# Query pieces of a weight-streaming kernel: one 512-column product and one 256-column product in place of three of 256 columns

## What is computed

```python
def peer(h, w_query, sub_keys, u_experts, v_experts):
    tokens = h.reshape(B * S // PEER_CHUNK, PEER_CHUNK, D)
    def chunk(xc):
        qh = (xc @ w_query).reshape(PEER_CHUNK, PEER_HEADS, PEER_QDIM)
        s1 = jnp.einsum('thd,hnd->thn', qh[..., :PEER_HALF], sub_keys[:, 0])
        s2 = jnp.einsum('thd,hnd->thn', qh[..., PEER_HALF:], sub_keys[:, 1])
        v1, i1 = lax.top_k(s1, PEER_TOPK)
        v2, i2 = lax.top_k(s2, PEER_TOPK)
        ...
        z = jnp.einsum('td,thkd->thk', xc, u_experts[idx])
        ...
```

## Time and profile before

| what | value |
|---|---|
| timed runs, median (lowest, highest) | 1732.64 us (1731.53, 1732.9) |
| profiled execution, span | 1732.8 us |
| TensorE matmul busy | 1711.1 us, 99% |
| weight loads busy | 1580.1 us, 91% |
| VectorE busy | 1328.8 us, 77% |
| ScalarE busy | 925.9 us, 53% |
| mean granted TensorE clock | 0.996 |

### The profile page before, as it was taken

How to read it: one execution, slowest core, us unless ns; L and a number is a source line. 1 busy time by engine, 2 the same in 40 slices (tenths; PEclk the granted TensorE clock), 3 DMA queues, 4 the chain that set the end, 5 groups by cost and what they waited for, 6 DMA issues and landing times.

```text
span 1732.8 us, 33390 instructions
## 1 busy us (share of the span) xinstructions
PE 1711.1 (99%) x11670; PEld 1580.1 (91%) x11670; DVE 1328.8 (77%) x2382; ACT 925.9 (53%) x1647; POOL 63.5 (4%) x112
## 2 busy tenths in 40 slices
PE   9999999999999999999999999999999999999997
PEld 8899899989999898999889999999999988888886
DVE  6986778778976787877775999987888766666666
ACT  5444544445454544455554555577777655555553
POOL 0000001000000122100000000000000000000000
PEclk9999999999999999999999999999999999999999
DMA  6556687755445699744344555554444455555554
GB/s 232 170 179 199 217 291 274 244 181 167 162 159 161 226 328 308 253 148 145 122 158 158 166 175 182 182 171 136 145 135 137 144 194 194 193 192 192 191 192 153
DMA packets 90123, 327.30 MB, mean 189 GB/s; under 512 B 11001, under 2 KB 11177, under 8 KB 89585
## 3 DMA queue, kind: packets, MB, share of 16 engines
q1 hardware_dynamic: 79056, 286.45, 49.3%
q0 software_dynamic: 9712, 34.36, 6.2%
q10 hardware_dynamic: 1264, 5.24, 0.8%
HBM read 323.88 MB, written 6.09 MB: 190 GB/s over the span
## 4 chain that ended last, share of the span: by engine, by line
PE 76%; DVE 18%; DMA 2%; issue 2%; ACT 2%; DVEq 0%; ACTq 0%; SPq 0%
PE bank L210 23%; PE bank L211 22%; PE bank L212 22%; DVE Z L87 6%; DVE w_lo L187 6%; PE bank L1769 3%; DMA raw<-stream 1%; DVE yc L87 1%; PE bank L281 1%; PE bank L1310 1%; ACT w_hi L182 1%; PE bank L481 1%; DVE work L87 1%; DVE rot L87 1%; DVE top L87 1%
## 5 line engine op out<-in xcount | busy, mean ns | idle before, releaser
L187 DVE TENSOR_TENSOR w_lo<-raw,w_hi 128x1024 fp32r<-128x1024 f32 x544 | 658.2, 1220 | 162.1 <-ACT w_hi L182 161.2
L182 ACT ACTIVATE w_hi<-raw 128x1024 fp32r<-128x1024 f32 x544 | 572.4, 1054 | 245.5 <-PE bank L212 163.2
L210 PE MATMUL bank<-u_hi,w_hi 128*128 128x256 f32 x2400 | 691.2, 288 | 1.7 <-DVE w_lo L187 0.8
L211 PE MATMUL bank<-u_lo,w_hi 128*128 128x256 f32 x2400 | 679.8, 283 | 0.0
L212 PE MATMUL bank<-u_hi,w_lo 128*128 128x256 f32 x2400 | 679.7, 283 | 0.0
L210 PEld LDWEIGHTS bank<-u_hi,w_hi 128*128 128x128 f32 x2400 | 460.9, 192 | 11.6 <-DVE w_lo L187 3.8
L211 PEld LDWEIGHTS bank<-u_lo,w_hi 128*128 128x128 f32 x2400 | 461.2, 192 | 2.2
L212 PEld LDWEIGHTS bank<-u_hi,w_lo 128*128 128x128 f32 x2400 | 460.7, 192 | 0.0
L210 PE MATMUL bank<-w_hi,a_hi 128*128 128x512 f32 x744 | 290.4, 390 | 0.0
L211 PE MATMUL bank<-w_lo,a_hi 128*128 128x512 f32 x744 | 290.1, 390 | 0.0
L212 PE MATMUL bank<-w_hi,a_lo 128*128 128x512 f32 x744 | 289.5, 389 | 0.0
(11 more groups left out here) (286 smaller groups left out, 1713.1 us busy)
## 6 DMA issues: line engine op xcount, KB each, us to landing
raw<-stream SPq DMA_DIRECT2D x544, 512.0 KB, 3.3
gate<-w_ada POOLq DMA_DIRECT2D x48, 512.0 KB, 6.4
t_rows<-t_by_distance POOLq DMA_DIRECT2D x8, 256.0 KB, 3.4
rpb_rows<-rpb_pad POOLq DMA_DIRECT2D x8, 224.0 KB, 3.9
bias_b<-rpb_rows POOLq DMA_DIRECT2D x16, 96.0 KB, 7.7
bias_a<-t_rows POOLq DMA_DIRECT2D x1, 1536.0 KB, 14.9
x<-x_in ACTq DMA_DIRECT2D x2, 512.0 KB, 5.8
gains_b<-gains POOLq DMA_DIRECT2D x1, 1024.0 KB, 9.0
```

The lines of the kernel that those rows point to most:

```text
L182: nc.scalar.activation(w_hi[:, s, :], raw[:, s, :], ACT.Copy).then_inc(s_hi, 1)
L187: nc.vector.tensor_tensor(w_lo[:, s, :], raw[:, s, :], w_hi[:, s, :].bitcast(F32), ALU.subtract).then_inc(s_split, 1)
L210: M.matmul(o, lh, rh, start=start, stop=False, skip_group_check=True)
L211: M.matmul(o, lh, rl, start=False, stop=False, skip_group_check=True)
```

## The change

`u_hi` and `u_lo` become the two halves of one tile, `u_hl`, so that for each k-step the high and the low part stand side by side as 512 columns. For the query pieces alone, three matmuls a k-step become two: `w_hi` times both parts in one matmul of 512 columns, which fills a whole bank, and `w_lo` times the high part, 256 columns, added to the bank's upper half. The result is the sum of the bank's halves: ScalarE copies the lower half out and VectorE adds the upper one to it. Each query piece has a bank of its own: q0 and q1 banks 4 and 5 as before, then bank `4 + (f + e - 1) % 4` for piece f + e, which is 5, 6, 7, 4, 5, 6, 7, 4 and so on for q2, q3, ... . All other products read `u_hi` and `u_lo` as views of the new tile.

```diff
-        u_hi = sb(ctx, "u_hi", [P, KD, T], F32R)
-        u_lo = sb(ctx, "u_lo", [P, KD, T], F32R)
+        u_hl = sb(ctx, "u_hl", [P, KD, 2, T], F32R)
+        u_hi, u_lo = u_hl[:, :, 0, :], u_hl[:, :, 1, :]
...
+        def mm_wide(o, lh, ll, both, start, stop):
+
+            M.matmul(o, lh, both, start=start, stop=False, skip_group_check=True)
+            return M.matmul(o[:, T:2 * T], ll, both[:, 0:T], start=False, stop=stop, skip_group_check=True)
+
+        def both_parts(k):
+            return u_hl[:, k, :, :].rearrange("p e n -> p (e n)")
+
+        def piece_wide(b):
+
+            s = next_piece()
+            take(b)
+            for k in range(KD):
+                w = slice(k * P, (k + 1) * P)
+                i = mm_wide(bank[b][:, :], w_hi[:, s, w], w_lo[:, s, w], both_parts(k), k == 0, k == KD - 1)
+            return used(i)
+
+        def halves_added(b, dst, m):
+
+            m1 = AC.go((m,), S.activation, dst, bank[b][:, 0:T], ACT.Copy)
+            m2 = VE.go((m1,), V.tensor_tensor, dst, dst, bank[b][:, T:2 * T], ALU.add)
+            free[b] = (m2,)
+            return m2
+
-        def two_pieces(outs, ready):
+        def two_pieces(outs, ready, wide=False):
...
-                    i = mm3(o, w_hi[:, s, w], w_lo[:, s, w], u_hi[:, k, :], u_lo[:, k, :], k == 0, k == KD - 1)
+                    if wide:
+                        i = mm_wide(o, w_hi[:, s, w], w_lo[:, s, w], both_parts(k), k == 0, k == KD - 1)
+                    else:
+                        i = mm3(o, w_hi[:, s, w], w_lo[:, s, w], u_hi[:, k, :], u_lo[:, k, :], k == 0, k == KD - 1)
...
-        pair = two_pieces([bank[4][:, 0:T], bank[5][:, 0:T]], h2_ready)
+        pair = two_pieces([bank[4][:, :], bank[5][:, :]], h2_ready, wide=True)
         for f in range(2):
-            m = AC.go((pair[f],), S.activation, qhT[:, f, :], bank[4 + f][:, 0:T], ACT.Copy)
-            free[4 + f] = (m,)
+            m = halves_added(4 + f, qhT[:, f, :], pair[f])
...
         for f in range(2, N_QUERY, 2):
-            b = 4 + (f // 2) % 2 if f > 2 else 6
-            take(b)
-            piece_b([bank[b][:, 0:T]], *U)
-            m = piece_b([bank[b][:, T:2 * T]], *U)
-            m = AC.go((m,), S.activation, qhT[:, f:f + 2, :].rearrange("p a n -> p (a n)"),
-                      bank[b][:, :], ACT.Copy)
-            free[b] = (m,)
+            for e in range(2):
+                b = 4 + (f + e - 1) % 4
+                m = halves_added(b, qhT[:, f + e, :], piece_wide(b))
             q_there.append(m)
```

## The result

The changed kernel takes 1736.26 us (median of 13 runs, 1733.43 to 1737.53) against 1732.64 us (13 runs, 1731.17 to 1733.14). The ratio is 1.0023, with a 95% interval of 1.0016 to 1.003: 3.6 us slower. The median lies just past the 0.2% that were named as the limit of what can be told, the interval on both sides of it. Measured again beside the experiments it was 1736.22 against 1732.83 us, a ratio of 1.002 (1.0011 to 1.0029). The forecast was 1735.6 us in a range of 1733.2 to 1737.4.

A forecast was written before the change was run, and what follows sets the result against it. TensorE was taken to bound the query stretch. Matmuls -1.65, wait for bank 5 +3.1 and clock +1.5 us sum to +2.95 us, giving 1735.6 us, 0.17% slower; range for 8 in 10 1733.2 to 1737.4 us.

The forecast's parts named there:

- What bounds: Query stretch: TensorE sets the pace, and a shift of the stretch's end reaches the end of the kernel unchanged.
- The wait for bank 5: Start of q2: TensorE waits for VectorE's add, queued behind the split of q4; +3.1 us, bounds 2.7 and 3.4.
- The rival without a wait: At q2: bank 5 is free in time or the wait is hidden, leaving only the saving; 1731.0 us, chance 0.05.
- The clock: Behind the wait for bank 5: granted clock falls to 0.5 for some 3.4 us; +1.5 us, bounds 0 and 1.6.
- The rival in which the clock holds: Behind the wait for bank 5: no fall of the granted clock; 1734.1 us, chance 0.17.
- The matmuls: 16 query pieces: each k-step goes from 359.4 to 346.5 ns, 12.9 ns less; -1.65 us in all.
- two widths in turn save nothing: Every k-step of the 16 pieces: all or most of the 1.65 us saving is missing; 1737.2 us, chance 0.13.
- gap formula: Query k-steps: columns / 2.4 GHz + 2.5 ns per matmul, saving 2.5 ns a k-step, 0.3 us over the stretch.
- Evictions, end and layout at nothing: Query pieces' copies and adds, the last key scores and the tile's gapped writes: no cost; layout between -0.1 and +0.5 us.
- The forecast's own range: Total time from the bounds of wait and clock: 1734.6 to 1736.6 us; the forecast case has chance 0.57.

The follow-up runs named there:

- the late split: The changed kernel with the split of q4 listed behind the evictions of banks 4 and 5 instead of ahead of them: 1733.09 us, ratio 1.0004.

## Why the prediction was right, and where its sizes were off

*What bounds.* Right. The loss of the stretch reached the end unchanged: 791.9 us behind it before, 791.7 after.

*The wait for bank 5.* Right in cause and size. Forecast q2 3.1 us late and 2.7 to 3.1 us of wait; q2 starts 12.37 us behind the transposing matmuls against 9.44 before (895.99 less 886.55), 2.93 us, and with the 0.1 us that q0 and q1 gained that is 3.0 us of delay, 2.87 us of it idle. The queue behind which the adds stood was named correctly: take one split out and the wait is 1.5 us, put one in and it is 4.0. The rival without a wait falls.

*The clock.* The mechanism was right: with TensorE busy in the wait there is no fall, after waits of 1.4 and 1.5 us there is none, after 2.9 there is one. The size, 1.5 us with bounds of 0 and 1.6, was measured at 1.3 us in one execution and is about 2.8 in the other (59.20 - 57.61 on top, less 0.1 us for one pair with the longer step). The step that failed is the upper bound: the trace of before had two falls, both of 3.4 us (rows 9 show the second only where it begins), and I took their length for a property of the clock. It isn't one: in the old kernel with the new bank the same wait of 2.4 us that led to 3.4 us at half clock elsewhere led to 6.8. Nor is a fall behind a wait of 2 us certain, as the late split's trace shows. What decides between no fall, a short and a long one is open. The rival in which the clock holds falls as the usual case; the one run of 1733.43 us, with the highest granted clock of the 13, may have been such an execution, but it has no profile.

*The matmuls.* The gain is there, but it is 1.2 us, not 1.65. The mis-sized term is the k-step: 346.5 ns was forecast from two plain streams, and in turn the two widths take 347 ns in some pieces and 353 in most (6.45 and 6.55 us for two pieces with a key score, where 6.43 was forecast). TensorE's timeline of the changed kernel, twice ten k-steps from start to start:

```profile
901.29 0.40 PE L228 MATMUL bank<-u_hl,w_hi 128*128 128x512 f32 x1
...
904.76 0.40 PE L228 MATMUL bank<-u_hl,w_hi 128*128 128x512 f32 x1
...
925.95 0.40 PE L228 MATMUL bank<-u_hl,w_hi 128*128 128x512 f32 x1
...
929.48 0.40 PE L228 MATMUL bank<-u_hl,w_hi 128*128 128x512 f32 x1
```

That is 347 and 353 ns, a saving of 12.4 or 6.4 ns a k-step, inside the bounds. The rival "two widths in turn save nothing" was half right in this and wrong in its price of 1.65 us. The Trainium skill's gap formula ("TensorE: Matmul & The Clock Gate", "Back-to-back issue gap"), which gave 0.3 us, is further from the 1.2 us than the rows were; the section gives it for an isolated matmul, and these are streams.

*Evictions, end and layout at nothing.* Right: with the wide matmul undone and all of these in place the stretch is 54.30 us against 54.32.

*The sum.* Forecast +2.95 us: -1.65, +3.1, +1.5. In the first profile: -1.1, +3.1 and +1.3 make 3.3, and the median shows 3.6. So 0.3 us of the 0.7 by which the median lies above the forecast are the saving that was 0.5 us too large, less 0.2 for the short fall; the rest would fit longer falls in some of the timed executions, which is not shown. That the time came out this near is in part luck: the median is of executions with a clock term of 1.3 and, it seems, of 2.8 us, and the forecast had 1.5. One slip stood in the conversion: the profiled execution of before was put 0.2 us from the median by its span, but an execution's time is 1.3 us above its span, so it was an execution of about 1734.1 us, slower than the timed ones. The forecast was made as a difference to the median and so didn't carry it. The forecast's own range, 1734.6 to 1736.6, doesn't follow from the bounds of wait and clock either: -1.65 + 3.4 + 1.6 us ends at 1736.0, below the 1736.26 that were measured. The chance of 0.26 for slower by over 0.2% was too low for a sum that stood 0.5 us from that limit with a clock term that could only be counted from two cases; the measured interval, 0.16 to 0.30%, doesn't say on which side of the limit the change lies.

## What to carry to other kernels

When buffers are dealt out anew, look at the first round by hand: a rotation that is roomy in the steady state can begin on the buffer that was filled last. The cost of such a wait is what the program has queued ahead of the release on each engine in its path, and an eviction that passes through two engines waits for the later of both queues (1.40 us here through ScalarE alone, 2.87 with VectorE behind it). The bank at which the rotation begins was worth 4.5 us in a change that saves 1.2 without it. A wait in the middle of a dense matmul stream has a second price in the clock, which a row of idle time doesn't show; ask whether the wait can be kept short, or filled.

## What was not expected of the hardware

- The granted clock stayed at half for 3.4 us in some falls and for 6.8 in others, behind the same wait of the same program. Behind a wait of 1.96 us it fell in nine traces and held in one.
- Matmuls of 512 and 256 columns in turn take 347 ns a pair in some stretches and 353 in others. Where the step changed it did so at a restart of the stream, behind the wait or behind key scores, and it held from there on; two of each width in turn gave 348.4 throughout.
